# First-block mixers of layers 1 and 2: a unit's attention starts within its value group, and the result is transposed later

## The reference

```python
def mixer_b(x, w_qkv, w_o, cos, sin):              # layer 1
    qkv = (x @ w_qkv).reshape(B, S, 3, 3, 16, 64)  # 3 dilations, q/k/v, 16 heads
    for g, (window, dil) in enumerate(((128, 1), (512, 4), (2048, 16))):
        q, k = apply_rope(qkv[:, :, g, 0]), apply_rope(qkv[:, :, g, 1])
        o, lse = dilated_attention(q, k, qkv[:, :, g, 2], window, dil)
    w = softmax(stack(lses), axis=0)
    return sum(w[..., None] * stack(outs)) @ w_o

def mixer_c(x, w_qkv, w_o, cos, sin):              # layer 2
    # 256 tokens are one block: causal attention over 16 heads
    return o.reshape(B, S, 1024) @ w_o
```

## Time and profile before

| | us |
|---|---|
| median of 3 runs | 2418.91 |
| lowest, highest | 2418.38, 2423.98 |
| the profiled execution | 2418.16 |
| its span in the profile | 2416.4 |
| TensorE busy | 2338.3 (97%) |
| VectorE, ScalarE, GpSimd busy | 1457.0, 1311.5, 332.5 |

### The profile page before, as it was taken

One profiled execution on the slowest core, in us unless ns is written; L12 is line 12 of the kernel. 1 busy time (PEld: TensorE's weight loads), 2 busy tenths in 40 slices (PEclk: granted clock), 3 DMA queues, 4 the chain that ended last, 5 costly groups with the idle time before them and its releaser, 6 DMA issues.

```text
span 2416.4 us, 36753 instructions
## 1 busy us (share of the span) xinstructions
PE 2338.3 (97%) x15344; PEld 2089.0 (86%) x15344; DVE 1457.0 (60%) x2241; ACT 1311.5 (54%) x1966; POOL 332.5 (14%) x307
## 2 busy tenths in 40 slices
PE   7999999998999999999999999989999999899999
PEld 6799888787899878998789988889899898898998
DVE  6655555555644547446765477565687675555875
ACT  5554465554544556445554466464655675555654
POOL 0100032211100313001010003413000023430000
PEclk9999999999999999999999999999999999999999
DMA  6255543333455534555255553334455543344553
GB/s 259 97 200 192 189 160 140 132 130 105 175 192 190 193 122 166 187 186 200 91 189 191 192 172 143 135 109 178 172 191 192 185 164 134 128 142 173 192 190 125
DMA packets 58182, 398.94 MB, mean 165 GB/s; under 512 B 6816, under 2 KB 7072, under 8 KB 11680
## 3 DMA queue, kind: packets, MB, share of 16 engines
q1 hardware_dynamic: 56864, 393.75, 45.1%
q10 hardware_dynamic: 1152, 2.83, 0.3%
HBM read 395.51 MB, written 1.05 MB: 164 GB/s over the span
## 4 chain that ended last, share of the span: by engine, by line
PE 59%; DVE 7%; ACT 5%; POOL 2%; issue 2%; ACTq 0%; DVEq 0%; POOLq 0%
PE b L1252 10%; PE b L1254 10%; PE b L1253 10%; PE b L1156 7%; PE b L1157 7%; PE b L1158 7%; PE b L1161 4%; DVE wlo L1908 3%; PE b L1165 2%; ACT whi L1549 2%; DVE xb L2201 1%; ACT b L1545 1%; PE b L1223 1%; PE b L1224 1%; POOL xn L2603 1%
## 5 line engine op out<-in xcount | busy, mean ns | idle before, releaser
L1908 DVE TENSOR_TENSOR wlo<-raw,whi 128x2048 fp32r<-128x2048 f32 x362 | 840.9, 2328 | 482.7 <-ACT whi L1549 482.2
L1549 ACT ACTIVATE whi<-raw 128x2048 fp32r<-128x2048 f32 x362 | 690.3, 1911 | 426.0 <-PE b L1254 240.9
L1252 PE MATMUL b<-xh,whi 128*128 128x256 f32 x2560 | 726.4, 284 | 0.8 <-DVE wlo L1908 0.8
L1254 PE MATMUL b<-xh,wlo 128*128 128x256 f32 x2560 | 714.9, 279 | 0.0
L1253 PE MATMUL b<-xl,whi 128*128 128x256 f32 x2560 | 714.1, 279 | 0.0
L1252 PEld LDWEIGHTS b<-xh,whi 128*128 128x128 f32 x2560 | 483.5, 189 | 6.1 <-DVE wlo L1908 2.7
L1253 PEld LDWEIGHTS b<-xl,whi 128*128 128x128 f32 x2560 | 484.3, 189 | 1.9
L1254 PEld LDWEIGHTS b<-xh,wlo 128*128 128x128 f32 x2560 | 483.8, 189 | 0.0
L1156 PE MATMUL b<-whi,xh 128*128 128x512 f32 x640 | 262.4, 410 | 1.5 <-DVE wlo L1908 1.5
L1156 PE MATMUL b<-whi,oh 128*128 128x512 f32 x656 | 259.7, 396 | 0.6 <-DVE ol L2192 0.6
L1157 PE MATMUL b<-wlo,oh 128*128 128x512 f32 x656 | 256.5, 391 | 0.0
(11 more groups left out here) (234 smaller groups left out, 2954.4 us busy)
## 6 DMA issues: line engine op xcount, KB each, us to landing
raw<-in_w SPq DMA_DIRECT2D x362, 1024.0 KB, 4.8
gt<-in_rows SPq DMA_DIRECT2D x8, 512.0 KB, 4.0
bt<-in_rows SPq DMA_DIRECT2D x8, 512.0 KB, 4.9
abq<-in_rows ACTq DMA_DIRECT2D x2, 768.0 KB, 6.0
x<-in_x SPq DMA_DIRECT2D x1, 1024.0 KB, 6.3
bc<-in_rows SPq DMA_DIRECT2D x4, 256.0 KB, 6.0
out<-x SPq DMA_DIRECT2D x4, 256.0 KB, 2.2
msk<-in_masks SPq DMA_DIRECT2D x1, 768.0 KB, 21.3
```

Of the source, the lines that this page charges most:

```text
L1252: pe.matmul(out, wh[:, k, cs], ah[:, kk, :], start=kk == 0 and s == 0, stop=False, skip_group_check=True)
L1254: last = pe.matmul(out, wl[:, k, cs], ah[:, kk, :], start=False, stop=final and k == 3, skip_group_check=True)
L1549: return ac.activation(out, i, ACT.Copy)
L1908: ve.tensor_tensor(B.wlo[r][:, :], B.raw[r][:, :], B.whi[s][:, :], ALU.subtract).then_inc(sem["loV"], 1)
```

## The change

The unit's attention is put in `side` ahead of the value group rather than behind it. It begins when q and k are transposed, and stops ahead of iteration 2 until the value group is done. The key's transposes come in the sixth pump of the value group rather than the seventh, and `done` is set one pump after a transpose. The `drain()` after each unit becomes a wait until the unit before is finished. `opart` of the first two pairs moves from the start of iteration 4 to that of iteration 5, and that of the others comes 7 side calls later (`hold=7`). In `project` of layers 1 and 2, the pump has n=5 rather than 6. Layers 0 and 3 and the second block keep their order (`hold=0`, n=6).

```diff
--- before.py
+++ after.py
@@ -517,7 +517,7 @@
 
         return a + v // 4, v % 4
 
-    def attention(self, a, n, mask, ready, consume, kidx, dv, sinks=None, tail=None, pace=7):
+    def attention(self, a, n, mask, ready, consume, kidx, dv, sinks=None, tail=None, pace=7, values=None, hold=0):
 
 
 
@@ -526,8 +526,10 @@
             if v % 4 == 0 and v < n:
                 while not ready(a + v // 4):
                     yield
-            for g in due[:1]:
-                tail(due.pop(0))
+            while v == 2 and values and not values():
+                yield
+            if due and due[0][1] < v - hold // 7:
+                tail(due.pop(0)[0])
             for i in range(2):
                 self.bank(("S", a, v, i), SB[i])
                 if 1 <= v <= n or v >= 2 and dv == 128:
@@ -563,10 +565,12 @@
                 if sinks is None:
                     consume(v - 2)
                 if v % 2 and tail is not None:
-                    due.append((v - 2) // 2)
+                    due.append(((v - 2) // 2, v))
             for _ in range(pace):
                 yield
-        for g in due:
+        for g, _ in due:
+            for _ in range(hold):
+                yield
             tail(g)
 
     def out_part(self, key, source):
@@ -585,13 +589,13 @@
             self.bank(("turn", key, t), TB[t])
             self.step("turn", key, t, buf, dst)
 
-    def project(self, name, layer, i, ready, boundary_of):
+    def project(self, name, layer, i, ready, boundary_of, n):
 
         a = 2 * i
         for blk in range(2):
             while blk not in ready:
                 self.pump()
-            self.drive(self.row_acc(name, layer, (blk,), a, "o", blk == 0), 6)
+            self.drive(self.row_acc(name, layer, (blk,), a, "o", blk == 0), n)
         while 2 not in ready:
             self.pump()
         end, finish = boundary_of(a, False)
@@ -601,7 +605,7 @@
                 yield
             self.drain()
             self.step("warm", a)
-        self.drive(self.row_acc(name, layer, (2, 3), a, "o", False, end, last_ready), 6)
+        self.drive(self.row_acc(name, layer, (2, 3), a, "o", False, end, last_ready), n)
         finish()
 
     def mixer_a(self, i):
@@ -653,7 +657,7 @@
                 ready[g] = True
             self.side.append(self.attention(u0, 8, "ma", lambda u: ("q", u) in turned, consume,
                                             lambda v, k: 2 * (v // 4) + (2 * (v % 4) + k) // 4, 64, 16 * j, tail))
-        self.project("a_w_o", j, i, ready, self.boundary)
+        self.project("a_w_o", j, i, ready, self.boundary, 6)
 
     def scale_x(self):
         for t in range(2):
@@ -670,25 +674,9 @@
                 u = self.units
                 self.units += 1
                 done = []
-                for p, part in enumerate("qkv"):
-                    self.drive(self.tok_out((part, u), name, 0, g * 3072 + p * 1024 + hh * 512, 2 * i,
-                                            hh + g + p == 0), 3)
-                    if part == "v":
-                        self.step("v_in", u)
-                        continue
-                    self.step("qk_in", part, u)
-
-                    def turned(part=part, u=u, done=done):
-                        self.rope((part, u), part, "one")
-                        for _ in range(6):
-                            yield
-                        self.turn((part, u), part, (part, u))
-                        done.append(part)
-                        yield
-                    self.pre.append(turned())
 
                 def heads(u=u, hh=hh, g=g, done=done):
-                    while len(done) < 2:
+                    while not {"q", "k"} <= set(done):
                         yield
 
                     def consume(gr):
@@ -707,10 +695,30 @@
                         self.out_part((i, 2 * hh + gr), hh if i == 2 else 0)
                         ready[2 * hh + gr] = True
                     yield from self.attention(u, 4, "mc" if i == 2 else f"mb{g}", lambda u: True, consume,
-                                              lambda v, k: v, 64, None, tail if i == 2 or g == 2 else None)
-                self.drain()
-                self.side.append(heads())
-        self.project("b_w_o" if i == 1 else "c_w_o", 0, i, ready, self.boundary)
+                                              lambda v, k: v, 64, None, tail if i == 2 or g == 2 else None,
+                                              values=lambda: "v" in done, hold=7)
+                for p, part in enumerate("qkv"):
+                    if part == "v":
+                        self.side.append(heads())
+                    self.drive(self.tok_out((part, u), name, 0, g * 3072 + p * 1024 + hh * 512, 2 * i,
+                                            hh + g + p == 0), 3)
+                    if part == "v":
+                        self.step("v_in", u)
+                        done.append("v")
+                        continue
+                    self.step("qk_in", part, u)
+
+                    def turned(part=part, u=u, done=done):
+                        self.rope((part, u), part, "one")
+                        for _ in range(6 if part == "q" else 5):
+                            yield
+                        self.turn((part, u), part, (part, u))
+                        yield
+                        done.append(part)
+                    self.pre.append(turned())
+                while len(self.side) > 1:
+                    self.pump()
+        self.project("b_w_o" if i == 1 else "c_w_o", 0, i, ready, self.boundary, 5)
 
 
 
```

## The result

| | before | changed |
|---|---|---|
| median of 20 runs, us | 2423.78 | 2418.68 |
| lowest, highest | 2417.74, 2427.08 | 2416.08, 2421.19 |
| span of the profiled execution | 2416.4 | 2416.9 |

The ratio is 0.9984, with a 95% interval from 0.9978 to 0.9991: a gain of 0.16%, or 3.9 us of 2423.78 (the two medians of the table lie 5.1 us apart). That is half of what I took as the least that one can tell from no change. With 20 runs each it can be told. The forecast was a gain of 2.6 us, and a median of 2416.3 us. The median is 2.4 us above that, because the forecast started from 2418.91 us, the median of only three runs of the kernel before, and that of 20 runs is 4.9 us higher. The profiled execution of before was among its fastest; the spans of the two profiles therefore don't show the gain.

A forecast was written before the change was run, and what follows sets the result against it. TensorE was taken as the bound, with gain only from its waits and low clock. Layer 1's −2.7 us and layer 2's +0.1 us gave −2.6 us, from 2418.91 to 2416.3 us, range 2409 to 2423 us.

The forecast's parts named there:

- What bounds it, and the size of the field: TensorE, busy 97% of the span; it is not busy for 18.4 us in the mixers of layers 1 and 2.
- The earlier start: Units: attention starts two pieces (2.7 us) sooner; no gain, key in time, cost 0, bounds 0 and 12 us.
- The first turn later: First half's results transposed later: waits shrink, gaining 1.0 us in layer 1's units and 1.6 us in layer 2.
- The projection: Layer 1's projection with n=5: waits of 5.7 us become 3.8 us; in layer 2, 0.22 us go.
- The price at `close`: First close in layers 1 and 2: a new wait for ol of 1.9 us each, bounds 1.5 and 4.
- The low clock behind the 3.14 us should go: Layer 1's projection: the low-clock stretch behind that wait vanishes, worth 1.7 us, bounds 0 and 3.4.
- Rival 2: The new wait at close, 3.2 us or more per layer, decides and time grows: +5.0 us, 2424 us; chance 0.18.
- Rival 1: Waits of iterations 3 to 5 and layer 1's low-clock stretches vanish: −8.1 us, 2411 us; chance 0.17.

The follow-up runs named there:

- e5: Kernel before with the earlier start alone (the change without hold, n=6): ratio 0.9987, median 2419.41 us.
- e4: Kernel before with only the first opart of a half moved to the start of iteration 5: ratio 0.9967, median 2414.65 us.
- e2: Changed kernel with the last opart of a half 3 side calls after the loop rather than 7: ratio 0.9945, median 2409.68 us.
- e8: e2 with the merge of pair v-2 put ahead of probs in units of layers 1 and 2: ratio 0.9945, median 2407.93 us.
- e6: Kernel before with only n=5 in the projections of layers 1 and 2: ratio 1.0026, median 2427.19 us.
- e3: Changed kernel with n=6 rather than 5 in the projections of layers 1 and 2: ratio 0.9966, median 2415.10 us.
- e9: Kernel before, no earlier start, n=6, first opart at iteration 5 and last one 3 side calls later: ratio 0.9955, median 2409.49 us.

## Why the prediction was right, and where not

**What bounds it, and the size of the field.** Right. The waits stand where the prediction named them, and TensorE's busy time changed by 1.3 us of 2338.

**The earlier start.** Right for the change as it is: no score waits for the key, the iterations keep their distances, and the second turn falls into the pump of the turn of q again, with its 0.83 us. What I missed is that the start by itself leaves 3.5 us fewer of waits (e5), of which 1.4 us only hid behind the low clock. 1.7 us are the two waits of 0.83 us, since it takes the last `opart` away from the turn of q. `hold=7` then puts it back there.

**The first turn later.** Right: 0.7 us were forecast for layer 1 and 0.67 are left; the 1.60 us of layer 2 went. e4 shows that this is the part that pays most.

**The projection.** 0.6, 2.4 and 0.8 us were forecast for iterations 3 to 5; 0.65, 2.31 and 0 us came. The 0.8 us failed in size. It was priced at the full clock. My reading is that the low stretch behind iteration 4 gave VectorE time. In the change's two profiles, e2 and e8, iteration 4 has a low stretch behind it and iteration 5 has no wait, so no run separates the two.

**The price at `close`.** 1.9 us forecast in each layer; 2.02 and 1.92 us came, from the cause named: `opart` right ahead, and a `lo` ahead of `ol`. The prediction's lower bound of 1.5 us is the hand-over alone (2.0 us less 0.5 us of transposes), which leaves 0.4 us for the `lo`; the rows above give it about 0.5 us.

**The clock.** Here a term failed: "The low clock behind the 3.14 us should go", worth −1.7 us, since 2.4 us was nearer to a wait behind which the clock had stayed full. In both profiles of the change the clock fell behind the 2.3 us wait, and once more behind `close`. One profile isn't enough to say that a wait of some length leaves the clock alone: behind layer 2's 2.41 us it was full in the first profile of before and low in the second. The one profile that the prediction had was the exception: behind layer 2's boundary the clock was low in nine of eleven. The mean clock of the runs doesn't show the gain either: 0.9891 over 11 runs of the change, beside 0.9894 over 15 of before. The term should have been a chance on every wait, and the sum then goes with the sum of the waits. That is what the table shows: for seven of the eight kernels the time moves by 1.3 to 1.9 us for each us of waiting by which it differs from before (e2: 0.55% of 2423 us is 13.3 us for 7.7 us; e6: 6.3 us for 4.1 us); e5 is at 0.9.

The clock on record makes up most of the difference. Fewer waits and what the clock saves, added, come within 1.5 us of the gain for every kernel of the table that has both (e2: 7.7 + 4.5 = 12.2 beside 13.3; e6: −4.1 − 2.7 = −6.8 beside −6.3; e5: 3.5 − 1.2 = 2.3 beside 3.2). The five kernels with the fewest waits (e2, e3, e4, e8 and e9) lost 1.5 to 5.0 us less to the low clock than before, and the one with the most (e6) lost 2.7 us more. The change and e5 lost no less than before.

So the agreement of the sum is in part luck. Without the clock, the prediction's terms came to 0.9 us less of waits, and 2.1 us less were measured, as iteration 5 no longer waits and some small waits went. The 1.7 us of the clock didn't come. The 2.1 us lie just under the interval of the gain, 2.2 to 5.3 us; what the rest is made of stays open, within the error of the clock's estimate.

**The rivals.** Rival 2's mechanism is there, with low stretches behind the new waits, but the price at `close` was 2.0 us and not 3.2 or more, so it didn't decide. Rival 1 came true only when the price was taken away (e2).

**The rule on the clock** that the Trainium skill gives (TensorE: Matmul & The Clock Gate, section "What's actually happening") says that the rate depends on how busy the array has been of late and that the observation doesn't restart with a kernel. The runs agree: in the two profiles of the change, with the same waits to 0.03 us, low stretches stood in different places in two executions. A slip in the prediction's reading stands beside it: the last waits ahead of layer 1's boundary were 19 and 23 us before it (0.32 and 0.22 us), and only those from 3.14 us back were 25 us and more.

## What to carry to other kernels

When a result is handed on through three engines (transposes, high part, low part: 2.0 us here), place its first step by the work that lies behind it on the bottleneck engine, not by how late its input is: the same delay that cured a wait of 1.5 us at the start of a half made one of 2.0 us at its end. Look, too, at which long operations (a rounding of 1.91 us, a subtraction of 2.28 us) stand ahead of its small copies. Try each part of a bundled change alone; here one of four edits was worth about twice the whole, and a constant of 7 rather than 3 cost 0.4%. Judge changes of a few microseconds by the sum of the waits on the bottleneck engine, which repeats to some hundredths but for waits behind a low stretch, beside the mean clock of many runs, and only then by the time, which spread over 9 us for the same kernel.

## What the runs showed of the hardware that I had not expected

A low stretch hides waits as well as costing time. In e5 the merge wrote og 7.1 us after the start of the `pv` before it, much as in the kernel before (6.9 us), but TensorE had run at 0.57 of its clock between, and waited 1.71 us rather than 3.14:

```profile
592.87 0.49 DVE L2170 TENSOR_TENSOR og<-b,wsm 128x128 f32<-128x128 f32 x2
```

In e3 and e4 the low stretch lay on the score ahead of the merge too: the two `pv` stood 8.7 and 8.6 us apart, and the wait was still 0.96 and 0.89 us rather than 2.3. So a wait and the low clock ahead of it must not both be counted in full.
